# GpSimd makes the low parts of two matrices' first steps, all of w_glu is split, GELU moves ahead of the q norm's exponential, bias and maximum are one instruction

## What is computed

```python
z = rmsnorm(x, attn_norm_g) @ w_in                 # q (16 heads of 64), k, v (4 heads), u (1024)
q, k = rmsnorm(q, q_norm_g), rmsnorm(k, k_norm_g)  # per head
s = q @ k.T * 64 ** -0.5 - slope[head] * delta     # window of 128, ALiBi
m = max(max(s), sink[head])
p = exp(s - m); p = p / (sum(p) + exp(sink - m)); attn = p @ v
y_ssm = scan(u) ...                                # complex diagonal state space, 64 groups
g = gelu(y_ssm)
ssm_out = g * sigmoid(g @ w_glu + b_glu)           # w_glu 1024 x 1024
h = x + concat(rmsnorm(attn), rmsnorm(ssm_out)) @ w_out
y = h + square(relu(rmsnorm(h, mlp_norm_g) @ w_mlp_up)) @ w_mlp_down
```

## Time and profile before

| | us |
|---|---|
| median of 3 runs | 1171.87 (1171.61 to 1173.36) |
| the profiled execution | 1171.93 |
| its span | 1170.1 |
| TensorE busy | 1163.9 |
| VectorE busy | 752.3 |
| ScalarE busy | 429.0 |
| GpSimd busy | 139.1 |

### The profile page before, as it was taken

One profiled execution on the slowest core, in us unless ns is written; L12 is line 12 of the kernel. 1 busy time (PEld: TensorE's weight loads), 2 busy tenths in 40 slices (PEclk: granted clock), 3 DMA queues, 4 the chain that ended last, 5 costly groups with the idle time before them and its releaser, 6 DMA issues.

```text
span 1170.1 us, 20365 instructions
## 1 busy us (share of the span) xinstructions
PE 1163.9 (99%) x8510; PEld 1100.1 (94%) x8510; DVE 752.3 (64%) x761; ACT 429.0 (37%) x520; POOL 139.1 (12%) x83
## 2 busy tenths in 40 slices
PE   9999999999999999999999999999999999999998
PEld 7676676899999999999999999999999999999998
DVE  7999999989765566544555555455654445555554
ACT  6110043885444343333334333334333333433331
POOL 0512603000000011000001000001100000100000
PEclk9999999999999999999999999999999999999999
DMA  7533334534544444545544555444455555445553
GB/s 293 188 128 108 131 122 145 167 102 154 192 166 165 164 158 151 192 165 171 169 163 145 167 189 167 162 163 161 146 180 178 165 174 165 145 164 183 174 164 118
DMA packets 55192, 190.29 MB, mean 163 GB/s; under 512 B 7864, under 2 KB 10168, under 8 KB 54712
## 3 DMA queue, kind: packets, MB, share of 16 engines
q1 hardware_dynamic: 54824, 188.79, 47.8%
q10 hardware_dynamic: 288, 0.30, 0.1%
HBM read 185.82 MB, written 5.28 MB: 163 GB/s over the span
## 4 chain that ended last, share of the span: by engine, by line
PE 98%; DVE 1%; DMA 1%; ACT 0%; SPq 0%; issue 0%; DVEq 0%
PE psum L1405 97%; DMA h_t<-in_x 1%; PE psum L1541 0%; DVE s_head L1083 0%; DVE w_lo L761 0%; ACT gate L631 0%; DVE q_t L1027 0%; DVE mov_b L770 0%; DVE stat L1088 0%; DVE q_blk L1161 0%; DVE stat L1087 0%; ACT x_g L482 0%; DVE t_b L770 0%; DVE h_t L770 0%; PE psum L1663 0%
## 5 line engine op out<-in xcount | busy, mean ns | idle before, releaser
L761 DVE TENSOR_TENSOR w_lo<-w_raw,w_hi 128x1024 fp32r<-128x1024 f32 x294 | 409.5, 1404 | 385.6 <-ACT w_hi L472 384.7
L1405 PE MATMUL psum<-mov_b,w_hi 128*128 128x288 f32 x2656 | 529.0, 295 | 0.2 <-ACT au L538 0.2
L472 ACT ACTIVATE w_hi<-w_raw 128x1024 fp32r<-128x1024 f32 x294 | 308.3, 1058 | 492.4 <-PE psum L1405 480.7
L1405 PEld LDWEIGHTS psum<-mov_b,w_hi 128*128 128x128 f32 x2656 | 424.9, 188 | 2.3 <-issue 1.0
L1405 PE MATMUL psum<-mov_a,w_hi 128*128 128x288 f32 x2048 | 406.6, 295 | 0.0
L1405 PE MATMUL psum<-mov_b,w_lo 128*128 128x288 f32 x1328 | 390.1, 294 | 0.0
L1405 PEld LDWEIGHTS psum<-mov_a,w_hi 128*128 128x128 f32 x2048 | 327.7, 188 | 0.1
L1405 PE MATMUL psum<-mov_a,w_lo 128*128 128x288 f32 x1024 | 300.7, 294 | 0.0
L1405 PEld LDWEIGHTS psum<-mov_b,w_lo 128*128 128x128 f32 x1328 | 250.6, 189 | 0.0
L1405 PEld LDWEIGHTS psum<-mov_a,w_lo 128*128 128x128 f32 x1024 | 193.3, 189 | 0.0
L1405 PE MATMUL psum<-x_g,w_raw 128*128 128x288 f32 x640 | 162.1, 410 | 1.0 <-DMA w_raw<-in_w 0.5
(11 more groups left out here) (182 smaller groups left out, 490.3 us busy)
## 6 DMA issues: line engine op xcount, KB each, us to landing
w_raw<-in_w SPq DMA_DIRECT2D x335, 512.0 KB, 3.3
h_t<-in_x SPq DMA_DIRECT2D x3, 576.0 KB, 9.4
out_y<-h_t SPq DMA_DIRECT2D x3, 576.0 KB
b_w<-in_b SPq DMA_DIRECT2D x1, 1024.0 KB, 7.6
c_w<-in_c SPq DMA_DIRECT2D x1, 1024.0 KB, 6.6
k_cache<-in_kc SPq DMA_DIRECT2D x1, 1024.0 KB, 5.4
v_cache<-in_vc SPq DMA_DIRECT2D x1, 1024.0 KB, 5.7
out_kc<-in_kc SPq DMA_DIRECT2D x1, 992.0 KB
```

What stands on the lines that cost most here:

```text
L472: nc.scalar.activation(hi3[:, n % SLOTS, :], raw3[:, n % SLOTS, :], ACT.Copy) \
L761: nc.vector.tensor_tensor(lo3[:, n % SLOTS, :], raw3[:, n % SLOTS, :], hi3[:, n % SLOTS, :].bitcast(F32), ALU.subtract) \
L1405: return nc.tensor.matmul(out, lhs_t, rhs, start=start, stop=stop)
```

## The change

- EARLY becomes all of steps 40 to 43, so glu0's steps 42 and 43 are split too; ScalarE makes hi_part(42) after waiting for the last turn_out (its slot of w_hi holds the tables of the scan until then) and hi_part(43) between the squares of q and u_his(0).
- The low parts of steps 40 to 43, of u's second half and of steps 44 to 51 are made by GpSimd instead of VectorE: 40, 41 and 42 each behind one of the last three copy_last, 43 behind the zero fill, then u's second half, then 44 to 51. VectorE keeps u's first half and the steps from 52 on.
- On ScalarE gelu(1) stands ahead of the exponential of the q norm, and u_his(1) ahead of exps(0).
- Biasing, multiplication with the slope, maximum and sink are one tensor_tensor_reduce for each block of keys (128 and 256 columns), eight for each soft_max and four for the sample scores. It computes (scores + delta) * slope, so q_norm divides q by the head's slope, with four instructions of 288 columns in place of one of 1152, and the sample bias holds distances alone.

```diff
-EARLY = (S_GLU, S_GLU + 1)
+EARLY = tuple(range(S_GLU, S_SPLIT))
+POOL_LOWS = 4
@@ scalar
             gelu(0)
-            for n in EARLY:
-                hi_part(n)
+            hi_part(EARLY[0])
+            hi_part(EARLY[1])
+            act.wait_ge(turned_out, 8)
+            hi_part(EARLY[2])
             unit_read(act, UNIT["g_q1"])
             for at in (0, 2):
                 nc.scalar.activation(au3[:, at:at + 2, :], q3[:, 4 + at:6 + at, :], ACT.Square).then_inc(squared, 1)
+            hi_part(EARLY[3])
             unit_full(act, UNIT["y1"])
             u_his(0)
             head_scale(UNIT["qn1"], au3, 4)
+            gelu(1)
             unit_read(act, UNIT["qn1"])
             nc.scalar.activation(au3, au3, ACT.Exp, scale=-0.5).then_inc(rsqrt_ready, 1)
-            gelu(1)
...
+            u_his(1)
             exps(0, 1)
-            u_his(1)
             hi_part(S_SPLIT)
@@ vector
             def q_norm(m, buf):
                 dve.wait_ge(rsqrt_ready, 2 + m)
-                nc.vector.scalar_tensor_tensor(q3[:, 4 * m:4 * m + 4, :], q3[:, 4 * m:4 * m + 4, :],
-                                               stat[:, 80:81], buf, ALU.mult, ALU.mult).then_inc(q_ready, 1)
+                for t in range(4):
+                    q = 4 * m + t
+                    scaled = nc.vector.scalar_tensor_tensor(q3[:, q, :], q3[:, q, :], stat[:, 80 + q:81 + q],
+                                                            buf[:, t, :], ALU.mult, ALU.mult)
+                scaled.then_inc(q_ready, 1)
...
-                    biased = nc.vector.scalar_tensor_tensor(sh4[:, s, b, :], delta, SLOPES[head],
-                                                            banks(u, 4, 384)[:, b, :], ALU.mult, ALU.add)
+                    for k, cols in ((0, slice(0, 128)), (1, slice(128, 384))):
+                        biased = nc.vector.tensor_tensor_reduce(
+                            sh4[:, s, b, cols], banks(u, 4, 384)[:, b, cols], delta[:, cols], SLOPES[head],
+                            small[:, sinks + b:sinks + b + 1], ALU.add, ALU.max,
+                            stat[:, at + 4 * k + b:at + 4 * k + b + 1])
                 biased.then_inc(evacuated[u % 2], 1)
                 unit_read(dve, u)
-                link(nc.vector.tensor_reduce(stat[:, at:at + 4], sh4[:, s, :, 0:128], A1210/1225/3158.X, ALU.max))
-                link(nc.vector.tensor_reduce(stat[:, at + 4:at + 8], sh4[:, s, :, 128:384], A1210/1225/3158.X, ALU.max))
-                linked()
-                link(tt(m, m, sink, ALU.max))
-                linked()
...
-            lo_part(EARLY[0])
-            u_los(0)
-            lo_part(EARLY[1])
+            dve.wait_ge(u_hi, 1)
+            tt(b4[:, 0:4, 1, :], u3[:, 0:4, :], b4[:, 0:4, 0, :].bitcast(F32), ALU.subtract).then_inc(u_lo, 1)
             soft_max(0)
...
-            lo_part(S_SPLIT)
-            lo_part(S_SPLIT + 1)
...
-            u_los(1)
-            lo_part(S_SPLIT + 2)
...
-            lo_part(S_WO + 3)
@@ gpsimd
+            def lo_part(n):
+                pool.wait_ge(hi_split, hi_count(n))
+                tt(lo3[:, n % SLOTS, :], raw3[:, n % SLOTS, :], hi3[:, n % SLOTS, :].bitcast(F32), ALU.subtract) \
+                    .then_inc(lo_split[n % SLOTS], 1)
...
             for half in range(2):
                 add_turned(half)
-                copy_last(half)
+                for o in range(4):
+                    copy_last(half, o)
+                    if half and o:
+                        lo_part(EARLY[o - 1])
             pool.wait_ge(last_copied, 8)
             unit_full(pool, UNIT["y1"])
             nc.gpsimd.memset(q_blk[:, :], 0.0).then_inc(q_blk_zero, 1)
+            lo_part(EARLY[3])
+            pool.wait_ge(u_hi, 2)
+            pool.wait_ge(u_lo, 1)
+            tt(b4[:, 4:8, 1, :], u3[:, 4:8, :], b4[:, 4:8, 0, :].bitcast(F32), ALU.subtract).then_inc(u_lo, 1)
+            for n in range(S_SPLIT, S_WO + POOL_LOWS):
+                lo_part(n)
@@ tensor
             def glu(m, tiles):
-                if m == 0 and tiles.stop <= STEP_K * len(EARLY):
-                    gemm(UNIT["glu0"], S_GLU, HALF_STEPS, b4, ready=tiles_ready(u_lo, per=4), part=tiles)
-                elif m == 0:
-                    gemm_full("glu0", S_GLU, HALF_STEPS, u3, tiles_ready(gelu_ready, per=4), tiles)
-                else:
-                    gemm(UNIT["glu1"], S_SPLIT, HALF_STEPS, b4, ready=tiles_ready(u_lo, per=4), part=tiles)
+                gemm(UNIT[f"glu{m}"], S_GLU + HALF_STEPS * m, HALF_STEPS, b4, ready=tiles_ready(u_lo, per=4), part=tiles)
```

More of the change, by code:

```diff
@@ L172, in build_program @@
         ssq_s, _ = sb("ssq_s", TOK)
-        stat, _ = sb("stat", 81)
+        stat, _ = sb("stat", 80 + QT)
         last_0, _ = sb("last_0", 2 * HALF_PAIRS * 9)
@@ L934, in _ @@
             link(nc.vector.tensor_scalar(ce4[:, 1, 1, :], ce4[:, 1, 0, :], -1.0, None, ALU.mult))
-            link(nc.vector.tensor_scalar(stat[:, 80:81], small[:, SMALL["g_q"]], HEAD_DIM ** -0.5, None, ALU.mult))
+            link(nc.vector.tensor_scalar(stat[:, 80:80 + QT], small[:, SMALL["inverse_slope"]], small[:, SMALL["g_q"]],
+                                         HEAD_DIM ** -0.5, ALU.mult, ALU.mult))
             linked()
@@ L1079, in soft_max @@
                     unit_full(dve, UNIT[f"pt{i - 2}"])
+                sinks = SMALL["sinks"].start + 4 * i
                 for b in range(4):
@@ L1119, in sample_max @@
                 bias = sample_bias[:, :].rearrange("p (b s) -> p b s", b=4)
-                tt(ss3, banks(u, 4, SAMPLE_KEYS), bias, ALU.add).then_inc(evacuated[u % 2], 1)
+                sinks, slopes = SMALL["sink_rows"].start, SMALL["slope_rows"].start
+                for b in range(4):
+                    g = b // 2
+                    biased = nc.vector.tensor_tensor_reduce(
+                        ss3[:, b, :], banks(u, 4, SAMPLE_KEYS)[:, b, :], bias[:, b, :], small[:, slopes + g:slopes + g + 1],
+                        small[:, sinks + g:sinks + g + 1], ALU.add, ALU.max, stat[:, 64 + b:65 + b])
+                biased.then_inc(evacuated[u % 2], 1)
                 unit_read(dve, u)
-                link(nc.vector.tensor_reduce(stat[:, 64:68], ss3, AX.X, ALU.max))
-                linked()
                 sink = small[:, SMALL["sink_rows"]].unsqueeze(2).to_broadcast([P, 2, 2])
-                m = stat[:, 64:68].rearrange("p (g b) -> p g b", g=2)
-                link(tt(m, m, sink, ALU.max))
-                linked()
                 link(nc.vector.tensor_scalar(stat[:, 68:72], stat[:, 64:68], -1.0, None, ALU.mult))
@@ L1359, in add_turned, with copy_last @@
                     tt(im, im, turn4[m % 2][:, :, 1, :], ALU.add).then_inc(turn_added, 1)
-            def copy_last(half):
-                for o in range(4):
-                    k = 4 * half + o
-                    js = slice(4 * o, 4 * o + 4)
-                    pool.wait_ge(turned_out, k + 1)
-                    tt(last4[half][:, :, js, 0], st5[:, LAST_CHUNK, :, js, CHUNK - 1],
-                       ot6[:, k % 2, :, LAST_CHUNK, :, CHUNK - 1], ALU.add)
-                    tt(last4[half][:, :, js, 1:9], st5[:, NCHUNK - 1, :, js, DEC_SEQ - 1:CHUNK:DEC_SEQ],
-                       ot6[:, k % 2, :, NCHUNK - 1, :, DEC_SEQ - 1:CHUNK:DEC_SEQ], ALU.add) \
-                        .then_inc(last_copied, 1)
+            def lo_part(n):
+                pool.wait_ge(hi_split, hi_count(n))
+                tt(lo3[:, n % SLOTS, :], raw3[:, n % SLOTS, :], hi3[:, n % SLOTS, :].bitcast(F32), ALU.subtract) \
+                    .then_inc(lo_split[n % SLOTS], 1)
+            def copy_last(half, o):
+                k = 4 * half + o
+                js = slice(4 * o, 4 * o + 4)
+                pool.wait_ge(turned_out, k + 1)
+                tt(last4[half][:, :, js, 0], st5[:, LAST_CHUNK, :, js, CHUNK - 1],
+                   ot6[:, k % 2, :, LAST_CHUNK, :, CHUNK - 1], ALU.add)
+                tt(last4[half][:, :, js, 1:9], st5[:, NCHUNK - 1, :, js, DEC_SEQ - 1:CHUNK:DEC_SEQ],
+                   ot6[:, k % 2, :, NCHUNK - 1, :, DEC_SEQ - 1:CHUNK:DEC_SEQ], ALU.add) \
+                    .then_inc(last_copied, 1)
             for half in range(2):
                 add_turned(half)
-                copy_last(half)
+                for o in range(4):
+                    copy_last(half, o)
+                    if half and o:
+                        lo_part(EARLY[o - 1])
             pool.wait_ge(last_copied, 8)
@@ L1818, in _lay_out @@
     put("sinks", np.broadcast_to(sinks[heads], (P, N_HEADS)))
+    inverse = (1.0 / np.array(SLOPES))[heads].reshape(QT, 2)
+    put("inverse_slope", np.repeat(inverse.T, HEAD_DIM, axis=0))
+    slopes = np.array(SLOPES).reshape(2, 2, Q_PER_KV)
+    put("slope_rows", np.broadcast_to(slopes[None, :, :, :, None], (4, 2, 2, Q_PER_KV, DEC_SEQ))
+        .transpose(0, 2, 3, 4, 1).reshape(P, 2))
     by_row = sinks.reshape(2, 2, Q_PER_KV)
@@ L1874, in _sample_bias @@
```

(5 more changed lines are left out.)

15 lines of the change are left out of this document (1 added, 14 removed).

## The result

The changed kernel takes 1180.0 us (median of 6 runs, 1178.55 to 1180.61) against 1171.91 (1171.52 to 1173.36) for the kernel before in the same session: ratio 1.0066, 95% interval 1.0056 to 1.0077. Its profiled execution took 1180.61 with a span of 1178.8, 8.7 more than before. It is slower, as forecast, and by 2.8 us more than the 1177.2 of the forecast.

The account below looks back on a forecast made before the run. TensorE, busy 1163.9 of 1170.1 us, was taken as the bound. 1171.93 + 6.7 (later sample scores) - 1.7 (TensorE's work) + 0.3 (waits behind) = 1177.2 us; own range 1175.8 to 1178.9, wide range 1173.3 to 1180.8.

Parts of the forecast that it names:

- TensorE's own work: glu0's four last k tiles go from plain float32 to split form, 8.20 to 6.48 us: -1.7 us.
- GpSimd and VectorE exclude each other: VectorE instructions with two SBUF tensors take turns with GpSimd's, whole instructions; a split step holds VectorE up to 2.3 us.
- Step A: Third and fourth turning: GpSimd's first split step delays the last turning, giving TensorE a new wait of 1.6 us.
- Step B: To the first GLU tile: the q norm's logarithm ends at 203.9, so glu0 starts 2.75 us late.
- Step C: To the sample scores: late exponential, held fourth q_norm(1) piece, eight fused instructions of 3.0; start +6.7 us, A to C.
- rival 3: Fused instructions run slower than a column a cycle or readout exceeds 0.3 each: 1178.7, both 1181; chance 0.10.
- Step D: Behind the sample scores: the rms_s sum has 1.6 us reserve under a hold up to 2.4; +0.3 (0 to 0.8).
- rival 4: TensorE's clock falls to 1.2 GHz behind its wait of over 4 us: +2.5 us, 1179.7; chance 0.15.
- Rivals 1: GpSimd's low part of u asks too late to hold q_norm(1), all four pieces go through: 1174.9; chance 0.15.
- Rivals 2: GpSimd doesn't get in between VectorE's instructions because VectorE asks first: 1171.8 to 1172.4; chance 0.10.

Follow-up runs that it names:

- experiment 1: The changed kernel plus eight zero-weight matmuls in TensorE's hole before the sample scores: 1177.57 us, ratio 1.0048.
- experiment 2: The changed kernel with the q norm's exponential ahead of gelu(1) again: 1179.51 us, ratio 1.0065.
- experiment 9: Experiment 8's kernel with biasing of scores 0 fused, sample biasing before probability scaling, and the turned probabilities' copy before the samples' exponentials: 1174.59 us, ratio 1.0014.
- experiment 8: The kernel before with all of w_glu's first half split, GpSimd making two low parts, u's second high part before the first softmax exponentials: 1172.7 us, ratio 1.0004.
- experiment 4: The changed kernel with GpSimd's low part of u's second half waiting until VectorE has copied the block queries: 1177.51 us, ratio 1.0047.
- experiment 5: The changed kernel with every low part made by VectorE again, none by GpSimd: 1174.56 us, ratio 1.0021.
- experiment 10: Experiment 9's kernel with the biasing of scores 2 ahead of the samples' scaling and the gate ahead of step 45's high part: 1170.52 us, ratio 0.9987.

## Why the prediction was right, and where not

- **TensorE's own work, -1.7**: right in kind; measured -0.72 (4.64 for 5.36 from the sample scores to the turned probabilities, experiment 1) and -0.81 (3.35 for 4.16 from there to scores 2) make -1.5.
- **GpSimd and VectorE exclude each other, one instruction at a time**: right, and wider than the rows of before could show. A GpSimd step of 1024 columns takes 2.36 (estimated 2.38).
- **Step A**: right. TensorE waits 1.41 and starts its last projection 1.60 later; 1.6 was forecast.
- **Step B**: right, 2.75 for 2.75.
- **Step C**: right, 6.79 for 6.7, by the path described: exponential to 208.52 (208.6), the fourth piece held, eight fused instructions 2.7 (3.0). Pieces of 128 and 256 columns follow each other at 0.27 and 0.40 with the readout of 0.08 in it; nothing of rival 3 came true. In the count, q_norm(1) starts 3.14 later, is held 2.39, and 0.4 and 0.8 come from the pieces and the fused instructions.
- **Step D**: too small. Four kernels, profiled without the second fall, wait 0.51 to 0.58 for rms_s, where I took 0.3 out of 0 to 0.8. In the changed kernel's profile the second fall hides it: TensorE itself is late.
- **Where the size was off: rival 4.** It had a chance of 0.15 and was the truth. Its price, +2.5, was right (2.3). What failed is its weight: the hole of over 4 us stood in my own sum, and "no row of this trace shows such a fall" was no argument, since no row of it has a hole of over half a microsecond there. The Trainium skill, "TensorE: Matmul & The Clock Gate", section "Part 1: The HAM clock gate (the "warmup" mystery)", has idleness bring the half clock; this trace agrees (0.50 at the hole of 4.52), though two other profiles keep the full clock at holes of 3.12 and 2.11. With that rule taken as the forecast, the time would have been 1179.7. The second fall, 1.6 at rms_s, was in no case of mine.
- So, in the profiled run: 5.3 forecast + 2.3 + 1.6 = 9.2, which is what TensorE's timeline shows at rms_s. The 5.3 itself is right by parts that cancel: 6.8 - 1.5 measured, for 6.7 - 1.7 + 0.3. For the median, without the second fall, I estimate 1171.9 + 6.8 - 1.5 + 2.3 (first fall) + 0.55 (rms_s) = 1180.05 from the figures above; 1180.0 was measured. So of the 2.8 us that the forecast was low 2.3 are the clock, some 0.25 Step D and 0.2 TensorE's saving. Rivals 1 and 2 didn't occur: GpSimd did ask in time, and did get in.
- **The range**: the forecast's own, 1175.8 to 1178.9, doesn't hold 1180.0; the wide one, 1173.3 to 1180.8, does because it was drawn over rival 4. The ends of the narrow one don't follow from its terms either: biasing 2.4 and no loss in D make 1176.3, biasing 4.5 and a loss of 0.8 make 1179.2.

## What to carry to other kernels

A subtraction that is given to GpSimd holds whatever VectorE next does from SBUF to SBUF, a copy or an operation on 8 columns as much as a long one; place it where VectorE reads PSUM or reduces, by a wait if need be. Before you move an operation ahead of another, list what is queued behind both and which bank each of those frees: the misses of experiments 2 and 9 were banks, and so was one of the waits of experiment 8. And if a sum contains a new hole of TensorE of 2 us or more, put the half clock behind it into the forecast: in five of the seven such holes profiled here it came.

## What the runs showed of the hardware

- TensorE's granted clock fell from 2.4 to 1.2 GHz within holes of 4.52 us (twice) and 0.6 to 1.5 us behind the end of holes of 4.03, 2.12 and 2.04, not with holes of 3.12 and 2.11 in two other profiled runs, and with none of 1.4 or less. Runs of one kernel differ in it (the six of the changed kernel, experiments 1, 4 and 5). It isn't only the new holes: of 27 runs of the kernel before seven took 1173.1 to 1173.7 at a mean clock of 0.999, the other twenty, all but one at 1.000, 1171.5 to 1172.6. The two falls that could be priced cost 2.3 us (6.8 us at 1.2 GHz, with the end of the hole in it) and 1.6 us.
- It also fell without a hole, 0.5 to 0.8 us behind the end of the 2.8 us of sample values (64 of its 72 matmuls have 16 columns), in three of the thirteen profiled runs, all of which have that stage. The cause stays open.
- A GpSimd subtraction that waits for a VectorE instruction takes its turn right behind it, also where VectorE's next instruction follows without a gap, every time it was seen. Held by it, besides tensor operations: copies from SBUF (3.02 for 0.73) and, in the changed kernel, a tensor_scalar on 8 columns:

```profile
233.93 1.91 DVE L1102 TENSOR_SCALAR stat<-stat 128x8 f32<-128x8 f32 x1
```

- Not held: the fused instruction with one input in PSUM, and in the version of experiment 10 the biasing of scores 1 (1.95) and the reductions behind it (0.69, 1.21) beside a GpSimd subtraction of 2.7 us.
